# Diagonal blocks as column tiles in the triangular inverses of a fused two-block kernel

## The reference

```python
a = jnp.where(strict, jnp.einsum("bhncd,bhnjd->bhncj", k_beta, k) * decay, 0.0)
t_inv = lax.linalg.triangular_solve(eye + a, jnp.broadcast_to(eye, a.shape),
                                    left_side=True, lower=True)
u = jnp.einsum("bhncj,bhnjv->bhncv", t_inv, v_beta)
```

## Time and profile before

| | us |
|---|---|
| median of 3 runs (lowest, highest) | 1737.94 (1737.22, 1738.88) |
| the profiled execution's own time | 1741.18 |
| its span in the profile | 1739.4 |
| PE busy | 1622.0 (93%) |
| DVE, ACT, POOL busy | 1126.3, 908.4, 455.6 |
| mean granted TensorE clock | 0.96 of full |

### The profile page before, as it was taken

The page is one execution under the profiler, slowest core; times in us unless marked ns, Lnnn a source line. Parts: engine busy times, 40 slices in busy tenths (PEclk is TensorE's granted clock), DMA queues, the critical chain, the costliest instruction groups (busy, mean ns, idle before and its releaser), DMA issues. The chain is left out here.

```text
span 1739.4 us, 26942 instructions
## 1 busy us (share of the span) xinstructions
PE 1622.0 (93%) x11064; PEld 1490.3 (86%) x11064; DVE 1126.3 (65%) x1830; ACT 908.4 (52%) x1477; POOL 455.6 (26%) x293
## 2 busy tenths in 40 slices
PE   6999999998999988899998889899998988989999
PEld 6889999887999876799987769799987777879997
DVE  3666665554779867577986656576656656667664
ACT  5653455335444455544446557466645646556652
POOL 1322342332544200045423232012211144012220
PEclk9999999999999998999999889999998988999999
DMA  6332121223888732398882300545542220155550
GB/s 256 123 122 74 65 82 67 80 97 139 335 337 325 261 139 97 113 359 334 328 318 73 102 21 25 219 169 174 190 170 85 98 73 25 63 228 180 184 180 38
DMA packets 40011, 276.09 MB, mean 159 GB/s; under 512 B 4560, under 2 KB 4688, under 8 KB 8400
## 3 DMA queue, kind: packets, MB, share of 16 engines
q1 hardware_dynamic: 39888, 274.37, 43.0%
HBM read 273.31 MB, written 1.05 MB: 158 GB/s over the span
## 5 line engine op out<-in xcount | busy, mean ns | idle before, releaser
L520 ACT ACTIVATE wh<-ring 128x1024 fp32r<-128x1024 f32 (+4 forms) x428 | 438.0, 1028 | 489.5 <-PE ps L542 482.9
L528 DVE TENSOR_TENSOR wl<-ring,wh 128x1024 fp32r<-128x1024 f32 (+3 forms) x364 | 451.2, 1244 | 356.2 <-ACT wh L520 351.6
L540 PE MATMUL ps<-hTh,wh 128*128 128x256 f32 x1904 | 552.4, 290 | 5.5 <-POOL hTl L679 2.9
L541 PE MATMUL ps<-hTl,wh 128*128 128x256 f32 x1904 | 543.5, 285 | 0.0
L542 PE MATMUL ps<-hTh,wl 128*128 128x256 f32 x1904 | 543.4, 285 | 0.0
L540 PEld LDWEIGHTS ps<-hTh,wh 128*128 128x128 f32 x1904 | 367.7, 193 | 11.7 <-issue 11.3
L541 PEld LDWEIGHTS ps<-hTl,wh 128*128 128x128 f32 x1904 | 368.2, 193 | 0.0
L542 PEld LDWEIGHTS ps<-hTh,wl 128*128 128x128 f32 x1904 | 367.6, 193 | 0.0
L536 POOL TENSOR_TENSOR wl<-ring,wh 128x1024 fp32r<-128x1024 f32 x64 | 171.8, 2685 | 604.8 <-ACT wh L520 604.8
L1375 DVE SCALAR_TENSOR_TENSOR arena<-arena 128x1024 f32<-128x1024 f32 x96 | 162.0, 1703 | 1.7 <-DMA arena<-in_ws 1.7
L540 PE MATMUL ps<-wh,acts 128*128 128x512 f32 x366 | 144.8, 396 | 0.3 <-DVE wl L528 0.3
(11 more groups left out here) (444 smaller groups left out, 2403.5 us busy)
## 6 DMA issues: line engine op xcount, KB each, us to landing
ring<-in_ws SPq DMA_DIRECT2D x197, 1024.0 KB, 4.9
arena<-in_ws SPq DMA_DIRECT2D x48, 1024.0 KB, 8.4
ring<-in_ws SPq DMA_DIRECT2D x5, 768.0 KB, 4.5
ring<-in_ws SPq DMA_DIRECT2D x4, 512.0 KB, 3.7
cst<-in_cst SPq DMA_DIRECT2D x1, 1731.0 KB, 8.9
ring<-in_ws SPq DMA_DIRECT2D x2, 780.0 KB, 4.4
rowt<-in_rowp SPq DMA_DIRECT2D x2, 610.0 KB, 5.8
x_sb<-in_x SPq DMA_DIRECT2D x2, 512.0 KB, 4.1
```

The lines of the kernel that those rows point to most:

```text
L520: ac.act(unit_hl(u)[0], unit_src(u), ACT.Copy).then_inc(*W.a(("hi", u)))
L528: ve.tt(l, unit_src(u), h, OP.subtract).then_inc(*W.v(("lo", u)))
L540: pe.mm(o_, lh, rh, start=start, stop=False)
L541: pe.mm(o_, lh, rl, start=False, stop=False)
```

## The change

A helper `blocks_mm` multiplies only the diagonal blocks: four products of 32 weight columns by 32 columns (levels 1 to 4), or two of 64 by 64 (level 5), each over all 128 rows, written to the PSUM partitions and columns of its block. What lies outside the blocks in the bank stays as the transposes of the level before left it, which is zero there. At level 6 only one quadrant is computed, 64 weight columns by 64, and DVE subtracts just that quadrant. In the RWKV mixer the XT step of level 1 stays whole. So of 72 steps 70 change: 46 to tiles of 32 columns, 12 to two tiles of 64, 12 to one quadrant.

In `plan_` the delta rule's groups get new starts (22.0, 27.8, 37.7, 44.1 in place of 22, 29.6, 37.2, 44.8 ticks), and the last steps of a group are 0.517 ticks apart in place of 0.475.

```diff
+        def blocks_mm(pe, o_, lhs, rhs, l):
+
+            w = 32 if l < 5 else 64
+            for c in [slice(w * j, w * j + w) for j in range(128 // w)]:
+                m = pe.mm(o_[c, c], lhs[:, c], rhs[:, c], start=True, stop=True)
+            return m
...
+        EARLY, LATE = slice(0, 64), slice(64, 128)
...
-                        m = pe.mm(bank[t][:, h, :], AT[t][:, h, :], X[t][:, h, :], start=True, stop=True)
+                        if l < 6:
+                            m = blocks_mm(pe, bank[t][:, h, :], AT[t][:, h, :], X[t][:, h, :], l)
+                        else:
+                            m = pe.mm(bank[t][LATE, h, EARLY], AT[t][:, h, LATE], X[t][:, h, EARLY], start=True, stop=True)
...
-                        m = pe.mm(bank[t][:, h, :], S_[t][:, h, :], XT[t][:, h, :], start=True, stop=True)
+                        if l < 6:
+                            m = blocks_mm(pe, bank[t][:, h, :], S_[t][:, h, :], XT[t][:, h, :], l)
+                        else:
+                            m = pe.mm(bank[t][EARLY, h, LATE], S_[t][:, h, EARLY], XT[t][:, h, LATE], start=True, stop=True)
...
-                    ve.tt(XT[t], XT[t], bank[t], OP.subtract).then_inc(*S.v((sg, "XT", l, t)))
+                    r, c = (EARLY, LATE) if l == 6 else (slice(0, 128), slice(0, 128))
+                    ve.tt(XT[t][r, :, c], XT[t][r, :, c], bank[t][r, :, c], OP.subtract).then_inc(*S.v((sg, "XT", l, t)))
...
-                        m = pe.mm(v4(b_[t])[:, h, :], BY[t][:, h, :], BXT[t][:, h, :], start=True, stop=True)
+                        if lv == 1:
+                            m = pe.mm(v4(b_[t])[:, h, :], BY[t][:, h, :], BXT[t][:, h, :], start=True, stop=True)
+                        elif lv < 6:
+                            m = blocks_mm(pe, v4(b_[t])[:, h, :], BY[t][:, h, :], BXT[t][:, h, :], lv)
+                        else:
+                            m = pe.mm(v4(b_[t])[EARLY, h, LATE], BY[t][:, h, EARLY], BXT[t][:, h, LATE], start=True, stop=True)
...
-        d_at, d_by = 22, 0.475
-        ds = len(delta_steps(0))
+        GDNT = dict(e0=22.0, e1=27.8, e2=37.7, e3=44.1, by=0.475, tail_by=0.475, post_by=0.517)
...
-            *[(d_at + 0.01 + d_by * (ds * (sg // 2) + ds / 2 * (sg % 2)), d_by, delta_steps(sg)) for sg in range(4)])
+            *[(GDNT[f"e{sg}"] + 0.01 + dat[i], dby[i], delta_steps(sg)[dcut[i]:dcut[i + 1]]) for sg in range(4) for i in range(3)])
```

More of the change, by code:

```diff
@@ L2460, in rw_t @@
                     for h in range(4):
-                        m = pe.mm(v4(a_[t])[:, h, :], BP[t][lv % 2][:, h, :], BX[t][:, h, :], start=True, stop=True)
+                        if lv < 6:
+                            m = blocks_mm(pe, v4(a_[t])[:, h, :], BP[t][lv % 2][:, h, :], BX[t][:, h, :], lv)
+                        else:
+                            m = pe.mm(v4(a_[t])[LATE, h, EARLY], BP[t][lv % 2][:, h, LATE], BX[t][:, h, EARLY], start=True, stop=True)
                     m.then_inc(*S.t(("Y", lv, t)))
@@ L2583, in rw_v @@
                     ve.wait_ge(*S.t["XT", lv, t])
-                    ve.tt(BXT[t], BXT[t], v4(b_[t]), OP.subtract).then_inc(*S.v(("XT", lv, t)))
+                    r, c = (EARLY, LATE) if lv == 6 else (slice(0, 128), slice(0, 128))
+                    ve.tt(BXT[t][r, :, c], BXT[t][r, :, c], v4(b_[t])[r, :, c], OP.subtract).then_inc(*S.v(("XT", lv, t)))
             yield "Hv"
@@ L2940, in build_program @@
         plan_ += of("n0", [("k", k) for k in range(8)]) + of("ba", [0])
-        d_at, d_by = 22, 0.475
-        ds = len(delta_steps(0))
+        GDNT = dict(e0=22.0, e1=27.8, e2=37.7, e3=44.1, by=0.475, tail_by=0.475, post_by=0.517)
+        dcut = [0] + [next(i for i, x in enumerate(delta_steps(0)) if ("e0", k) in x) for k in ("VN0", ("sq", 1))] + [len(delta_steps(0))]
+        dby = [GDNT["by"], GDNT["tail_by"], GDNT["post_by"]]
+        dat = [sum(dby[j] * (dcut[j + 1] - dcut[j]) for j in range(i)) for i in range(3)]
         halves = lambda n: [(m, k) for m in range(n) for k in range(2)]
```

## The result

| | before | after |
|---|---|---|
| median of 4 runs each, us | 1738.41 | 1692.88 |
| lowest and highest | 1737.22, 1750.95 | 1683.04, 1694.09 |
| the profiled execution's own time | 1741.18 | 1691.88 |
| its span | 1739.4 | 1690.1 |
| mean granted TensorE clock | 0.96 | 0.96 |

The ratio is 0.971, with a 95% interval of 0.9652 to 0.9767: 45 us faster. A later series with six runs of the same changed kernel gave 1688.03 us and 0.9695 [0.9665, 0.9726]; so two versions under 5 us apart are not told apart here by single medians. The forecast was 1692.

A forecast was written before the change was run, and what follows sets the result against it. PE, busy for 93% of the span, was taken as the bound. Gains of 34 us (delta rule) and 12 (RWKV), 46 together, took 1741.18 to 1695; the median lying 3.2 lower gave 1692, range 1674 to 1738.

The forecast's parts named there:

- What bounds a step: In a level's step, weight load sets the pace (0.112 us a pass), not streaming; fewer weight columns and side-by-side tiles count.
- rival 1: Tiles in steps not side by side, 0.112 us a set: 1738 us, or about 1725 by the skill's 25 ns rule; chance 0.12.
- rival 2: In the steps a set of four passes costs 0.133 us, as in line 2395: 1769 us; chance 0.09.
- The size of a step's gain: Gain of 1.08 us on each of 46 steps and 0.66 on 24, together 65.5 us of PE's time.
- leaving costs nothing: At a step's end, going from tiles to full products adds no time; a drain there would cost 6 us in all.
- The set of 0.032: In steps of 32 columns, each set of four tile passes (one head, one pass) takes 0.032 us.
- What takes it back: In the delta rule, waits return 7 us for DVE in the levels and 4 us for the groups' starts.
- The new ticks at nothing: The delta rule's new group ticks cost nothing, between 4 us of gain and 5 us of loss.
- Delta rule, 34 us: Gain in the delta rule's stretch: 45 us of steps less 7 and 4 us of waits.
- RWKV, 12 us: Gain in the RWKV levels: 60% of 20.4 us, with ACT and DVE nearly full beside a shorter PE.
- rival 4: Narrow tiles lower PE's clock in RWKV and a tenth of the delta rule, about 20 us: 1712 us; chance 0.05.
- rival 3: DVE, ACT and POOL become the bound; 40% of the delta rule's gain and 30% of RWKV's arrive: 1714 us; chance 0.12.

The follow-up runs named there:

- e7: Changed kernel with tile and head loops swapped, so four products in a row use the same array columns: 1714.55 us, one execution.
- e8: Changed kernel with tiles of 32 weight columns, streaming 64, at levels 5 and 6 too: 1690.15 us, 0.9703 of before.
- e1: Changed kernel's column tiles with the delta rule's groups and steps at the old ticks: 1705.03 us, 0.9787 of before.
- e2: Kernel before with the new ticks but no column tiles, all products full 128x128: 1739.24 us, 0.9978 of before.
- e3: Changed kernel with tiles in the delta rule alone, the RWKV mixer as before: 1719.71 us, 0.9861 of before.
- e5: Changed kernel with the fourth of eight products in each delta-rule Y and XT step full (tiles, full, tiles): 1706.24 us, one execution.
- e9: The changed kernel again, unaltered, timed for the later series: 1688.03 us, 0.9695 of before.
- e10: Changed kernel with the new group starts, but the last steps of a group 0.475 ticks apart again: 1693.05 us, 0.9723 of before.
- e11: e8's tiles, with groups 1 and 3 started one tick earlier still (26.8 and 43.1): 1696.46 us, 0.9742 of before.
- e12: e8's tiles, with the RWKV inverse steps 1.0 ticks apart in place of 1.1: 1711.06 us, 0.9817 of before.
- e4: Changed kernel with two tiles of 64 columns in place of four of 32 at levels 1 to 4: 1711.37 us, 0.9832 of before.
- e6: Changed kernel with the last of eight products in each delta-rule Y and XT step full (tiles, full): 1692.91 us, one execution.

## Why the prediction was right, step by step

**PE is the bound and gives its time back: right.** By the steps PE's work shrank by 53 us (below), and the span by 49.3. The signs that I named came weaker: busy time down by 57.5 us for "60 us or more", idle time up by 8.2 for "15 to 20", steps of 0.90 and 1.28 us for 0.7 and 1.1.

**What bounds a step: right as far as it decided.** Tiles side by side are what pays (e7); that the streamed columns would not matter was true of full-width weights only and not of tiles (e8); rival 1 (serial tiles) and rival 2 (0.133 a set) fell with the 0.90 us of a step. The same rows tell of the rule that stood beside rival 1: 64 starts in 0.56 us are 9 ns each, and even in e7 it is 21. The Trainium skill, TensorE: Matmul & The Clock Gate, Part 1, has about 25 ns as the least distance of two starts; the measurement decides, and it is less here.

**The size of a step's gain: too large, by three parts.**

| step of 32 columns, us | predicted | measured |
|---|---|---|
| last projection to first tile pass | 0.206 | 0.209 |
| from there to the last pass (predicted: the last set) | 0.027 + 15 x 0.032 = 0.507 | 0.567 |
| from there to the next full load | 0 | 0.124 |
| sum | 0.71 | 0.90 |

The step that failed is "leaving costs nothing". It came from the earlier trace rows, transpositions with 16 columns between full products; their two passes start 0.115 us apart like those of full products, not side by side like tiles, and I read them as a case of leaving. The drain is there: 0.12 us after 32 columns, 0.15 after 64, on 70 steps 9 us. The set of 0.032 was right for the first half of a step; a change of rhythm behind it (the last section) adds 0.03 us and the starts within the last set, which I had left out, 0.03, together 3 us on 46 steps. For 64 columns the sets were right (0.93 for 0.056 + 15 x 0.058 = 0.926) and only the leaving was missing: 1.28 in place of 1.13. So the work saved is 46 x 0.89 + 24 x 0.505 = 53 us and not 65.5; in the delta rule 36.6 and not 45.1. The stretch's work fell by 304.8 - 267.4 = 37.4.

**What takes it back, 11 us in the delta rule: right in sum for the old ticks, e1, and not in its parts.** There the idle time grew by 25.2 - 15.5 = 9.7 us. Of the 7 us for DVE in the levels 3.3 came (lines 1140 and 1145 against 1126 and 1130), of the 4 us for the groups' starts 3.0, and 2.1 are waits that the profile puts down to no engine ("issue"), which I had not foreseen (the last section has such gaps). With the new ticks the idle time grew by 0.7. I also misread the 5.3 us of the earlier trace rows: they are not one wait for each of the four groups, but two at the first (3.3 us) and one of 1.0 at the third and the fourth, so three later starts at 1.8 us are 3.4 us more than they paid.

**The new ticks at nothing: wrong.** My reason was a gain of 4 us for POOL's wait against a loss of 5. Beside the tiles they are worth 14 us in the stretch (e1 to after: 9.0 idle, 3.4 clock, 1.9 work), and 10 without them (e2: 4.6 idle, 6.9 clock, less 1.2 work). Of the waits that the old starts leave bare behind short steps the new ones take away 2.0 us at the groups' starts, 2.8 at POOL's norm, 1.9 at the masks and 1.2 at ACT's copies. I costed the two edits apart from each other, with the chains priced at their old places.

**Delta rule, 34 us: 38.4.** 37.4 of work, less 0.7 idle, plus 1.7 clock (13.7 less 10.2 at the lower level, halved). The tiles' term was 8.5 us too large, and for waits and ticks together I had taken off 11 us where 1 us was gained (the idle time and the clock): 12 us too much. These cancel but for 4 us.

**RWKV, 12 us: 9.9 between these two traces.** By the steps 14 x 0.89 + 8 x 0.505 = 16.5 us were saved, and 9.9 arrived, 60%. But e3 shows that this difference of two traces is itself a matter of where the clock falls: taken out alone, these tiles were worth 20 us or more. What supports the share of 60% is e3's split without the clock: 15.5 us of work saved, 5.5 lost to idle time.

**The clock.** It stayed at 0.96 as forecast, so rival 4 fell as stated. **DVE as the next bound** (rival 3): PE waits 1.6 us for lines 1140 and 1145 together; it fell.

The total, 1692.88 for 1692, owes its closeness to luck as well: the two errors in the delta rule have opposite signs, and the 3.2 us that I took off because the profiled execution before lay above the median hid the rest (for the profiled execution I had 1695, it took 1691.88, and this time it lay 1.0 below the median). The mechanism was right; its terms were off by 8 to 14 us each.

## What to carry to other kernels

Small products on different column groups of the array run side by side; keep passes of one group apart in the order, and put all of them into one run between full products, since each further run of tiles costs 0.29 us at its two ends. Price a cost at a mode's edge from rows that are themselves in that mode. When steps get shorter, the starts of the dependent chains have to be placed anew with them, and the two edits priced together: the new ticks took 4.6 us of idle time from the delta rule with full products and 9.0 with tiles, and in the whole program they were worth a quarter to a third of the gain (12 to 17 of 45 to 50 us).

## What the runs showed of the hardware that was not expected

**A run of narrow passes changes its rhythm after 33.** In the single records of a step of the kernel after, the second set of four starts 52 ns after the first, and the next seven 32 ns apart, which brings it to the 33rd pass. From the 34th on the starts come late and in pairs: the sets take 42 and 49 ns, and the rest 33 each. So do the steps of the delta rule that no wait breaks; where a wait breaks one after 32 passes, the other 32 keep 32 ns a set. So do those of e5, which has a full product after the 24th tile pass and 32 tile passes behind it (0.46 - 0.196 = 0.26 us for all). The change costs 0.03 us a step. The Trainium skill, TensorE: Matmul & The Clock Gate, Part 3, gives TensorE a window of 64 instructions, and 32 passes with their loads are 64; whether this is the cause was not tried.

**A gap in the middle of a step.** One step of the kernel after stops for 1.7 us after 50 passes, with no wait of the program behind it:

```profile
293.74 0.65 PE L548 MATMUL ps<-arena 128*32 128x32 f32 x50
296.03 0.33 PE L548 MATMUL ps<-arena 128*32 128x32 f32 x14 [1.65 <-issue]
```

e8 has it at the same pass of the same step:

```profile
292.17 0.65 PE L549 MATMUL ps<-arena 128*32 128x32 f32 x50
294.57 0.33 PE L549 MATMUL ps<-arena 128*32 128x32 f32 x14 [1.76 <-issue]
```

Four times as many instructions in a step need to be brought to PE; the profile's queue for instructions moves 1.74 MB in 106 packets, before 1.43 MB in 87. The records point at these packets. In the kernel after the last pass before the gap starts at 294.19, and a packet of 16384 bytes of this queue is on its way from 293.54 to 294.43. e3, e8, e9, e10, e11 and e12 have such a gap too, and in each a packet starts 2.2 to 2.5 us before PE goes on and lands 1.3 to 1.6 us before it. In after, e3, e9 and e10 the same 7320 loads and passes stand ahead of the gap, in e8 and e12 exactly 512 more. e4, with half as many instructions in a step, and e7, with as many at less than half the pace, have none; nor have e5 and e6, and e1 has none within a run of tiles. That a packet is too late for PE here is likely, but no run was made to show it.

**The clock moves 8 us about.** The same code of the first RWKV layer took 153.2, 160.6 and 161.2 us (before, e2, e3), with 34.1, 51.4 and 51.4 us at the lower level. And within the runs of e4, one program, three took 1711 us at a mean clock of 0.955 or 0.956 and one 1719.5 at 0.945.
